# Scan stage of a state-space block: normed rows split into two f16 parts before they are turned, and one engine empties the turn bank

## The reference, cut to what matters

```python
y = ssd(xs, dt, a, bm, cm)                      # chunks of 128 tokens, 4 groups of 8 heads
y = y + d_skip[:, None] * xs
y = y.reshape(bsz, s, SSM_D_INNER) * jax.nn.silu(z_ssm)
y = rms_norm(y.reshape(bsz, s, 4, 512), ssm_norm_g.reshape(4, 512)).reshape(bsz, s, SSM_D_INNER)
y_ssm = y @ w_branch_ssm
```

## Time and profile before

| | us |
|---|---|
| median of 3 runs | 2694.79 (2691.94 to 2696.42) |
| span of the profiled execution | 2688.0 |
| scan stage of group 0, first to last instruction on PE | 1908.28 to 2019.6 |
| PE busy, share of the span | 2438.2 (91%) |
| DVE busy, share of the span | 1630.9 (61%) |
| ACT busy, share of the span | 1036.7 (39%) |
| POOL busy, share of the span | 661.3 (25%) |

### The profile page before, as it was taken

One profiled execution on the slowest core, in us unless ns is written; L12 is line 12 of the kernel. 1 busy time (PEld: TensorE's weight loads), 2 busy tenths in 40 slices (PEclk: granted clock), 3 DMA queues, 4 the chain that ended last, 5 costly groups with the idle time before them and its releaser, 6 DMA issues. The chain is left out here.

```text
span 2688.0 us, 38899 instructions
## 1 busy us (share of the span) xinstructions
PE 2438.2 (91%) x14919; PEld 1267.4 (47%) x14919; DVE 1630.9 (61%) x2819; ACT 1036.7 (39%) x1597; POOL 661.3 (25%) x676
## 2 busy tenths in 40 slices
PE   4999995998799999399989998798999999999999
PEld 3556544554455555245434444344444444444444
DVE  7787776222223223557497999844765757747863
ACT  6111453121112222555464648713533524614620
POOL 2011020000000000332254522100731712703702
PEclk8999897999999999699899999899999999999999
DMA  8786658899999998320002319643002002020133
GB/s 246 199 290 167 232 172 285 318 391 388 384 390 377 383 349 333 122 72 24 32 24 71 110 71 199 155 171 118 9 1 102 9 20 83 9 83 28 63 118 126
DMA packets 207370, 451.87 MB, mean 168 GB/s; under 512 B 103600, under 2 KB 113200, under 8 KB 198768
## 3 DMA queue, kind: packets, MB, share of 16 engines
q1 hardware_dynamic: 171344, 368.02, 39.6%
q10 hardware_dynamic: 25696, 48.93, 5.2%
q0 software_dynamic: 10176, 32.78, 4.2%
HBM read 371.86 MB, written 58.94 MB: 160 GB/s over the span
## 5 line engine op out<-in xcount | busy, mean ns | idle before, releaser
L1490 PE MATMUL m_gu<-conv_y,m_xT 128*64 128x256 f32 x1024 | 233.6, 387 | 17.2 <-DMA arena<-in_moe_w_up 14.9
L2728 POOL TENSOR_TENSOR group_words<-group_words 128x1024 f16<-128x1024 f16 x64 | 149.8, 2361 | 373.3 <-PE i_pj L144 364.1
L1597 DVE TENSOR_TENSOR m_hid<-m_sg,m_gu 64x256 f32<-64x256 f32 x96 | 39.6, 412 | 319.8 <-ACT m_sg L1541 319.8
L1492 PE MATMUL m_gu<-arena,m_xT 128*64 128x256 f32 x1024 | 233.6, 388 | 0.0
L1492 PEld LDWEIGHTS m_gu<-arena,m_xT 128*64 128x64 f32 x1024 | 143.1, 140 | 73.8 <-issue 15.4
L1512 PE MATMUL m_y_ps<-arena,m_hidT 128*64 128x512 f32 x768 | 175.4, 598 | 0.0
L1541 ACT ACT_TABLE_LOAD x48 | 61.6, 1283 | 293.2 <-issue 293.2
L1490 PEld LDWEIGHTS m_gu<-conv_y,m_xT 128*64 128x64 f32 x1024 | 143.0, 140 | 35.3 <-issue 24.6
L142 PE MATMUL i_pj<-hT,group_words 128*128 128x512 f16 x384 | 146.5, 381 | 13.3 <-DVE group_words L357 7.6
L142 PE MATMUL s_pj<-hT,arena 128*128 128x512 f16 x368 | 141.6, 385 | 14.1 <-issue 14.0
L143 PE MATMUL i_pj<-hT,group_words 128*128 128x512 f16 x384 | 146.5, 382 | 0.0
(11 more groups left out here) (628 smaller groups left out, 6463.8 us busy)
## 6 DMA issues: line engine op xcount, KB each, us to landing
arena<-in_moe_w_down SPq DMA_DIRECT2D x32, 2048.0 KB, 24.4
conv_y<-in_moe_w_gate SPq DMA_DIRECT2D x22, 2048.0 KB, 17.0
arena<-in_moe_w_up SPq DMA_DIRECT2D x22, 2048.0 KB, 23.9
hT<-in_moe_w_gate SPq DMA_DIRECT2D x10, 2048.0 KB, 15.9
hT<-in_moe_w_up SPq DMA_DIRECT2D x10, 2048.0 KB, 21.6
x_tok<-in_ada_w ACTq DMA_DIRECT2D x8, 2048.0 KB, 12.2
slot_out<-m_y ACTq DMA_DIRECT2D x96, 128.0 KB, 8.1
arena<-in_w_gates SPq DMA_DIRECT2D x23, 512.0 KB, 4.1
```

The source lines that it names most:

```text
L1490: g = nc.tensor.matmul(gu_ps[i][g_rows, 0:FFN // 2], lhsT=xT[:, c, :], rhs=k.wg[e % WEIGHT_SLOTS][:, c, cols], start=c == 0, stop=c == KC - 1)
L1492: u = nc.tensor.matmul(gu_ps[i][u_rows, 0:FFN // 2], lhsT=xT[:, c, :], rhs=k.wu[e % WEIGHT_SLOTS][:, c, cols], start=c == 0, stop=c == KC - 1)
L1597: nc.vector.tensor_tensor(hid[:, i, :], sg[:, i, :], gu_ps[i][u_rows, 0:FFN // 2], ALU.mult) \
L2728: return tuple(k.nc.gpsimd.tensor_tensor(k.y_U[:, t % 2, n], k.adt_parts[:, n, t, heads].unsqueeze(2).to_broadcast([P, HPG, P]), k.upto16. ...
```

## The change

Row t - 1 is scaled and split while it still lies as tokens by channels: ACT makes `row_high` (f16, scaled by the reciprocal), DVE makes `row_low` (f16, one scalar_tensor_tensor, written over the first half of the row itself). PE then turns both with eight f16 turns into one bank of f16, and one ACT copy of 8x128 columns empties it into `yT`. The DVE operations L3227 and L3232 are gone. `row_high` lies in the memory of `sq`, so ACT's Square now waits for the turns before it. The turns stand on PE between `st_ps` and `z`; on ACT `silu_z` comes last in the chunk, and on DVE `split_row(t - 1)` comes ahead of `y` of chunk t. A fourth f16 constant, `ident16`, is made once by POOL.

```diff
--- before.py
+++ after.py
@@ -2716,7 +2716,8 @@
     last = 8 * D + 16
     k.y_sq, k.y_cbm = at(last, GW // 2).bitcast(BF16), at(last + GW // 2, 2 * P).rearrange("p (a l) -> p a l", a=2)
     k.adt_parts = at(last + 2 * P + GW // 2, TT * SSM_HEADS).bitcast(F16).rearrange("p (n t h) -> p n t h", n=2, t=TT)
-    k.upto16, k.after16 = (at(last + 2 * P + GW // 2 + TT * SSM_HEADS + n * P // 2, P // 2).bitcast(F16) for n in range(2))
+    k.upto16, k.after16, k.ident16 = (at(last + 2 * P + GW // 2 + TT * SSM_HEADS + n * P // 2, P // 2).bitcast(F16)
+                                      for n in range(3))
     k.w_z = k.yT[:, :, :, :].rearrange("p a c s -> p (a c s)").bitcast(F32).rearrange("p (c n) -> p c n", c=KC)
     k.w_first = k.w_branch[:, 4 * D:5 * D].rearrange("p (c q) -> p c q", c=KC)
     k.ws_branch = k.w_branch[:, 0:4 * D].bitcast(F16).rearrange("p (c a n) -> p a c n", a=2, c=4)
@@ -2796,7 +2797,8 @@
                 nc.gpsimd.tensor_tensor(k.adt_parts[:, 1], k.adt, wide, ALU.subtract).then_inc(parts, 1)
                 pool.wait_ge(parts, 4)
                 nc.gpsimd.tensor_scalar(k.adt_parts[:, 1], k.adt_parts[:, 1], -64.0, None, ALU.max).then_inc(parts, 1)
-                pool.wait_ge(parts, 5)
+                nc.gpsimd.tensor_copy(k.ident16, k.const("ident")).then_inc(parts, 1)
+                pool.wait_ge(parts, 6)
             pool.wait_ge(low, splits(4))
             pool.wait_ge(pj_done, 5)
             for t in range(2):
@@ -2966,10 +2968,12 @@
         cb = k.ps(f"y{g}_cb", [P, P], ctx=ctx)
         seg = k.ps(f"y{g}_seg", [P, HPG * P], ctx=ctx)
         yd_ps, yo_ps, st_ps = (k.ps(f"y{g}_{n}", [P, GW], ctx=ctx) for n in ("yd_ps", "yo_ps", "st_ps"))
-        tr, br = k.ps(f"y{g}_tr", [P, HALF], ctx=ctx), k.ps(f"y{g}_br", [P, HALF], ctx=ctx)
+        tr, br = k.ps(f"y{g}_tr", [P, 2, 4, P], F16, ctx=ctx), k.ps(f"y{g}_br", [P, HALF], ctx=ctx)
+        row_high = sq.bitcast(F16)
+        row_low = lambda t: k.z_ssm[:, t, 0:GW // 2].bitcast(F16)
         names = ("pool_in", "U_done", "seg_done", "cb_done", "E_done", "cbm_done", "M_done", "yd_done",
-                 "yo_done", "st_done", "state_done", "yo_read", "y_done", "gated", "squared", "std", "normed",
-                 "tr_done", "tr_high", "tr_low", "br_done", "br_out", "dve_step", "xd_done", "f_high", "f_low",
+                 "yo_done", "st_done", "state_done", "yo_read", "y_done", "gated", "squared", "std", "rstd", "row_high",
+                 "row_low", "tr_done", "turned", "br_done", "br_out", "dve_step", "xd_done", "f_high", "f_low",
                  "small", "z_done", "z_out")
         q = {n: k.sem(f"y{g}_{n}") for n in names}
 
@@ -3057,12 +3061,12 @@
 
             def transposes(t):
 
-                pe.wait_ge(q["normed"], t + 1)
                 if t:
-                    pe.wait_ge(q["tr_low"], t)
-                for c in range(4):
-                    last = nc.tensor.transpose(tr[:, c * P:(c + 1) * P], k.z_ssm[:, t, c * P:(c + 1) * P],
-                                               k.const("ident"))
+                    pe.wait_ge(q["turned"], t)
+                pe.wait_ge(q["row_low"], t + 1)
+                for n, row in enumerate((row_high, row_low(t))):
+                    for c in range(4):
+                        last = nc.tensor.transpose(tr[:, n, c, :], row[:, c * P:(c + 1) * P], k.ident16)
                 last.then_inc(q["tr_done"], 1)
 
             def branch(j):
@@ -3070,8 +3074,7 @@
                 if j == 0:
                     pe.wait_ge(q["z_out"], TT - EARLY_Z)
                 if j == 0 or j == KC:
-                    pe.wait_ge(q["tr_high"], 4 + a // P)
-                    pe.wait_ge(q["tr_low"], 4 + a // P)
+                    pe.wait_ge(q["turned"], 4 + a // P)
                 if before(j) is not None:
                     pe.wait_ge(q["br_out"], before(j) + 1)
                 elif j == 4:
@@ -3102,6 +3105,8 @@
                     if t + 1 < TT:
                         nc.tensor.matmul(st_ps[:, :], lhsT=k.B_tok[:, t, :], rhs=xds[:, s].rearrange("p h d -> p (h d)"),
                                          start=True, stop=True).then_inc(q["st_done"], 1)
+                    if t >= 2:
+                        transposes(t - 2)
                     if t + EARLY_Z < TT:
                         z(t + EARLY_Z)
                     if t in middle:
@@ -3115,9 +3120,9 @@
                                                     rhs=xdt[:, s, h, :], start=True, stop=True)
                             if h == HPG - 1:
                                 last.then_inc(q["yd_done"], 1)
-                elif t in middle:
-                    branch(middle[t])
-                if t >= 2:
+                else:
+                    if t in middle:
+                        branch(middle[t])
                     transposes(t - 2)
                 if t in end:
                     branch(end[t])
@@ -3142,19 +3147,25 @@
             for t in range(TT + 2):
                 if t + 1 < TT:
                     decay(t + 1)
-                if t + EARLY_Z < TT:
-                    silu_z(t + EARLY_Z)
                 if 1 <= t <= TT:
+                    if t >= 2:
+                        act.wait_ge(q["tr_done"], t - 1)
                     act.wait_ge(q["gated"], t)
                     nc.scalar.activation(sq, k.z_ssm[:, t - 1, :], ACT.Square,
                                          accum_out=ss[:, t - 1:t]).then_inc(q["squared"], 1)
                     act.wait_ge(q["squared"], t)
                     nc.scalar.activation(ss[:, t - 1:t], ss[:, t - 1:t], ACT.Sqrt, bias=eps[:, :],
                                          scale=1.0 / GW).then_inc(q["std"], 1)
+                if t > TT:
+                    act.wait_ge(q["tr_done"], t - 1)
                 if t >= 2:
-                    act.wait_ge(q["tr_done"], t - 1)
-                    nc.scalar.copy(yT[:, 0, :, (t - 2) * P:(t - 1) * P],
-                                   tr[:, :].rearrange("p (c q) -> p c q", q=P)).then_inc(q["tr_high"], 1)
+                    nc.scalar.copy(yT[:, :, :, (t - 2) * P:(t - 1) * P], tr[:, :, :, :]).then_inc(q["turned"], 1)
+                if 1 <= t <= TT:
+                    act.wait_ge(q["rstd"], t)
+                    nc.scalar.activation(row_high, k.z_ssm[:, t - 1, :], ACT.Copy, scale=ss[:, t - 1:t]) \
+                        .then_inc(q["row_high"], 1)
+                if t + EARLY_Z < TT:
+                    silu_z(t + EARLY_Z)
             if g + 1 < SSM_GROUPS:
                 act.wait_ge(next_in, 16)
                 act.wait_ge(q["seg_done"], TT - 1)
@@ -3166,6 +3177,14 @@
             v = nc.vector
             v.memset(eps[:, :], EPS).then_inc(q["small"], 1)
             dve.wait_ge(q["small"], 1)
+            def split_row(t):
+
+                dve.wait_ge(q["std"], t + 1)
+                v.reciprocal(ss[:, t:t + 1], ss[:, t:t + 1]).then_inc(q["rstd"], 1)
+                dve.wait_ge(q["row_high"], t + 1)
+                v.scalar_tensor_tensor(row_low(t), in0=k.z_ssm[:, t, :], scalar=ss[:, t:t + 1], in1=row_high,
+                                       op0=ALU.mult, op1=ALU.subtract).then_inc(q["row_low"], 1)
+
             def decayed(t):
 
                 s = t % 2
@@ -3209,6 +3228,8 @@
                         dve.sem_inc(q["yo_read"], 1)
                     if t + 1 < TT:
                         decayed(t + 1)
+                    if t:
+                        split_row(t - 1)
                     if t in middle:
                         accumulate(dve, middle[t])
                     dve.wait_ge(q["yd_done"], 2 * t + 2)
@@ -3219,19 +3240,11 @@
                         dve.wait_ge(q["z_out"], t - EARLY_Z + 1)
                     v.tensor_tensor(z, z, y[:, :], ALU.mult).then_inc(q["gated"], 1)
                     dve.wait_ge(q["gated"], t + 1)
-                elif t in middle:
-                    accumulate(dve, middle[t])
-                if 1 <= t <= TT:
-                    dve.wait_ge(q["std"], t)
-                    step(v.reciprocal(ss[:, t - 1:t], ss[:, t - 1:t]))
-                    v.tensor_scalar(k.z_ssm[:, t - 1, :], k.z_ssm[:, t - 1, :], ss[:, t - 1:t], None, ALU.mult) \
-                        .then_inc(q["normed"], 1)
-                if t >= 2:
-                    dve.wait_ge(q["tr_high"], t - 1)
-                    h = yT[:, 0, :, (t - 2) * P:(t - 1) * P]
-                    v.tensor_tensor(yT[:, 1, :, (t - 2) * P:(t - 1) * P],
-                                    tr[:, :].rearrange("p (c q) -> p c q", q=P), h, ALU.subtract) \
-                        .then_inc(q["tr_low"], 1)
+                else:
+                    if t == TT:
+                        split_row(t - 1)
+                    if t in middle:
+                        accumulate(dve, middle[t])
             accumulate(dve, end[TT + 1])
             for j in range(KC, 2 * KC):
                 accumulate(dve, j)
```

## The result

The changed kernel takes 2712.94 us, the median of 4 runs (2707.74 to 2715.40), against 2695.61 us for the kernel before (the three runs of its table and a fourth). The ratio on record is 1.0073, with a 95% interval of 1.0060 to 1.0087: slower by 16 to 23 us. (The two medians alone divide to 1.0064, 17.3 us.) The profiled execution has the lowest of the four times, 2707.74 us; the others are 4 to 8 us above it.

The account below looks back on a forecast made before the run. PE was taken to bound the kernel, with the POOL and DVE ring at 10.40 us a chunk holding it up. Four groups at 3.25 add 13 to the 2688.0 span; with 6.8 around it, 2707.8 us, range 2694 to 2714.

Parts of the forecast that it names:

- the ring of POOL and DVE: Scan chunks: POOL and DVE wait for each other, 10.40 us a turn against PE's 9.61; this case had 0.64.
- the wait of 1.30 given back before job 1: Before branch jobs: the 1.30 us before job 0 goes, but job 1 waits for DVE's later accumulate, returning it in full.
- The port: DVE and POOL in SBUF: blocked operations overlap by 0.14 us; holding the port throughout would make the ring 11.1.
- The turns: PE, each chunk: eight overlapping f16 turns take 0.44 us, 0.05 less than four f32 turns.
- rival C: PE's turns don't overlap, 1.76 us against 0.49: much slower, 2737 us or half of that; chance 0.09.
- ACT: ACT's chunk: larger copy and `row_high` make some 8 us, hidden under PE's 9.61.
- From `segments(7)` to job 1: End of a group's scan: job 1 starts 9.3 to 9.5 us after `segments(7)`, against 9.38 before.
- job 3: Branch jobs on PE: job 3 comes about 0.3 us late, since Square of row 6 waits for turns behind job 1.
- Rivals A and B: Whole kernel: A, ring under PE's pace, 2685.6 us, chance 0.10; B, no change, 2692 to 2700 us, chance 0.17.
- Four groups: **+13 us: Whole kernel: each group loses 2.9 + 0.05 + 0.3 = 3.25 us, four groups +13 us.
- Some 2: PE before branch job 1: a wait of some 2 us, released by DVE, as a sign of the forecast case.
- The 6.8 around the span: Outside the profiled span: 6.8 us takes 2688.0 to the median 2694.8, and was added to the forecast span 2701.0.

Follow-up runs that it names:

- the run with work in the wait: The changed kernel with nine extra f16 products of 128x512 on PE right before branch job 1: 2706.22 us, ratio 1.0050 to the kernel before.
- the longer wait in the kernel before: The kernel before, with DVE's accumulate of branch job 0 moved behind the sum and gate of chunk 6: 2703.39 us, ratio 1.0042.
- the run with `y` ahead: The changed kernel with `split_row` moved behind `y` and the gate on DVE: 2711.56 us, ratio 1.0063 to the kernel before.

## Why the prediction was off

The case forecast came: slower, by the ring of POOL and DVE, with the wait of 1.30 given back before job 1. The size did not. The median of 2712.94 is 5 us above the forecast of 2707.8; the ratio of 1.0073 times the 2694.8 of before is 2714.5, 7 us above it and just over the upper end of 2714. The forecast growth was 13 us, the span grew by 17.6, and the ratio says 19.7.

- **The ring**: forecast 10.40 us a chunk, measured 10.36. Its parts came too: 9.25 and 1.15 forecast, 9.20 and 1.15 measured. The U pair was forecast at 5.17 and is 5.17; `segments(7)` was to be 2.9 late and is 2.77.
- **The port**: the rows' overlap of 0.14 was preferred to the Trainium skill's whole instruction ("SBUF — State Buffer", Who interferes with whom, which says it of DVE's two-port modes). L3185 starts at 1948.30 and ends at 1949.74, 0.55 after U's end at 1949.19: 0.75 alone less 0.2. The forecast had the same 0.55 as 0.69 less 0.14, so two small misses cancelled there, which is luck. The measurement decides for the rows; a ring of 11.1 did not come.
- **The turns**: 0.44 forecast, 0.45 measured; rival C is out. The Trainium skill's 275 ns ("TensorE: Matmul & The Clock Gate", Part 4: PE-mode transpose) is not the pace of turns that stand in a row here: eight start within 0.45 us.
- **ACT**: hidden, as said; the copy took 0.99 and ended 1.97 us ahead of need.
- **From `segments(7)` to job 1**: 9.3 to 9.5 forecast, 9.58 measured; job 3 0.3 forecast, 0.38 measured. A group loses 3.37 us by its period where the clock held, against 3.25 forecast. Rivals A and B are out with that.
- **The step that failed** is the sum's last line, "Four groups: **+13 us**". It took PE's waits as waiting alone. The 1.30 and 0.69 that were there before and the 2.48 that took their place are not far apart in sum (1.99 and 2.48), but they are in what follows: behind the 2.48 the granted clock was at 1.2 GHz in two groups of the profiled execution, 1.46 us each. The mechanism of the ring was right, and the term for the clock was missing from the sum. It is 2.8 us at the jobs in this execution; another 1.85 came with a fall in the next inputs, which may be chance. Over all executions the run with work in the wait took back some 6 us by the ratios, and the longer wait in the kernel before cost 5 us beyond its length. "Some 2" before job 1 had even been forecast, and not followed to what PE's clock does behind it.
- **The 6.8 around the span** is wrong, without harm to the sum. In the changed kernel an execution is 2.1 us longer than its own span (2707.74 and 2705.6). With the same 2.1, the profiled execution of the kernel before took about 2690.1 (an estimate), 4.7 below its median of 2694.8. The profiled execution of the change is 5.2 below its own median, so both profiles show quick executions, and their difference of 17.6 is close to that of the medians, 17.3.
- **Against the median**: the other three executions were up to 7.7 us longer than the profiled one, at a mean granted clock of 0.955 to 0.959 against its 0.962. In the 29 runs of the kernel before on the second chip, too, the longer ones tend to have the lower clock (correlation -0.56). More falls of the clock would fit, but traces of those executions were not taken, so this is argued, not shown.

## What to carry to other kernels

Where the bounding engine is TensorE, sum its waits by place and not only by length: one wait of 2.5 us cost more here than two of 1.3 and 0.7, since products behind it ran at half pace in some groups. Some work put into the wait, or a cheap reordering of the engine that it waits for, gave that back. Two engines that pass values to each other and share a port form a ring, and the time of one turn of it must be worked out before an operation is put on it; freeing one operation of the ring only moved the meeting to the next here. When a change delays a release that stands in a list behind the new work, try the release ahead of it first: here that one move took back 14 of 20 us.

## What the runs showed of the hardware

- After PE had waited 1.97 to 2.94 us before a branch job, the granted clock was at 1.2 GHz in some groups and not in others: 10 of 16 in four kernels, two of four after an identical 2.48 us. After 3.68 us it was so in four of four, after 0.25 to 1.42 us in none (table above). Products of 512 columns then start 0.42 instead of 0.22 apart for about 3 us, 1.46 us lost. The Trainium skill ("TensorE: Matmul & The Clock Gate", Part 1) has the low clock as the default that activity lifts. The traces agree in that the clock is back at 2.4 GHz after some 3 us of products, and they show that one place can fall on either side.
- A single wait's length does not tell it all. At the start of the scan PE waits 0.94 and then 1.09 us with only a few products between, and there the clock fell in 10 of the 44 scans of the eleven traces, none of them in the two kernels compared. The row below is from the run with `y` ahead; the same four products take 1.04 at 2.4 GHz.

```profile
1910.77 1.89 PE L3045 MATMUL y_seg<-group_words 128*128 128x512 f16 x4 [1.09 <-ACT group_words L3139]
```

- A DVE operation with one f32 and one f16 input in SBUF waits for POOL's as those with two f32 inputs do (L3185: 1.44 beside U, 0.75 without; 0.75 beside U once an input is in PSUM).
- ACT's copy of 1024 columns out of PSUM (f16 in and out) took 0.99 us, less than twice the 0.57 of 512 columns (f32 in, f16 out).
